# Expert blocks of 96 tokens, with tokens 64 to 95 in four narrow column groups of TensorE

## What the reference computes

```python
logits = (h @ w_router) + b_router
topv, idx = lax.top_k(logits, 4)            # 4 of 32 experts for each of 512 tokens
gates = softmax(topv)
# for each expert e and the tokens x that chose it
gu = x @ w_gate_up[e] + b_gate_up[e]        # 1024 -> 2 x 1024
gate = minimum(gu[:, :1024], 7.0)
up = clip(gu[:, 1024:], -7.0, 7.0)
act = (up + 1.0) * (gate * sigmoid(1.702 * gate))
y = act @ w_down[e] + b_down[e]             # 1024 -> 1024
# out[token] += gate weight * y
```

## Time and profile before

| what | value |
|---|---|
| median of 3 runs | 3157.65 us (3156.02 to 3158.03) |
| profiled execution, from first to last instruction | 3155.9 us |
| median of the runs less that span | 1.75 us |
| TensorE busy in the span | 2956.2 us |
| VectorE, ScalarE, GpSimd busy | 1215.3, 751.5, 116.9 us |
| transfers of expert weights in the span | 384 of 1 MB |

### The profile page before, as it was taken

How to read it: one execution, slowest core, us unless ns; L and a number is a source line. 1 busy time by engine, 2 the same in 40 slices (tenths; PEclk the granted TensorE clock), 3 DMA queues, 4 the chain that set the end, 5 groups by cost and what they waited for, 6 DMA issues and landing times.

```text
span 3155.9 us, 43167 instructions
## 1 busy us (share of the span) xinstructions
PE 2956.2 (94%) x15320; PEld 2056.7 (65%) x15321; DVE 1215.3 (39%) x2572; ACT 751.5 (24%) x1483; POOL 116.9 (4%) x132
## 2 busy tenths in 40 slices
PE   8989899998999999899899879898999999999999
PEld 7874667655585556386357668586776596776774
DVE  6770773242212221211212156535333355444432
ACT  3221751111212121211211023514111225232111
POOL 0000100000000000000000000011000000110000
PEclk9999999988999999999999989899999999999999
DMA  4222012257999999999999452021321220112221
GB/s 171 81 67 79 3 41 80 74 204 298 395 364 365 419 413 390 416 379 382 408 415 391 149 201 95 1 87 49 108 84 54 100 95 27 61 61 87 81 80 67
DMA packets 137804, 577.60 MB, mean 183 GB/s; under 512 B 15981, under 2 KB 21485, under 8 KB 87504
## 3 DMA queue, kind: packets, MB, share of 16 engines
q1 hardware_dynamic: 128176, 558.87, 46.6%
q0 software_dynamic: 9504, 17.07, 1.4%
HBM read 572.47 MB, written 20.97 MB: 188 GB/s over the span
## 4 chain that ended last, share of the span: by engine, by line
PE 85%; DVE 5%; DMA 5%; ACT 2%; issue 2%; DVEq 1%; SPq 0%; POOLq 0%; ACTq 0%
PE banks L395 31%; PE banks L1521 13%; PE banks L1497 9%; PE banks L332 8%; PE banks L1027 7%; PE banks L1471 6%; DMA arena<-in_w_experts 5%; PE banks L800 3%; PE banks L823 2%; PE banks L811 2%; PE banks L271 1%; DVE arena L873 1%; DVE arena L885 1%; PE banks L1451 1%; PE banks L1926 1%
## 5 line engine op out<-in xcount | busy, mean ns | idle before, releaser
L395 PE MATMUL banks<-arena 128*128 128x256 f32 (+2 forms) x4704 | 1015.3, 377 | 21.6 <-ACT arena L432 7.4
L395 PEld LDWEIGHTS banks<-arena 128*128 128x128 f32 x4704 | 883.8, 192 | 142.0 <-issue 21.5
L1521 PEld LDWEIGHTS banks<-arena 128*128 128x128 f32 x3584 | 403.8, 193 | 14.5 <-issue 14.5
L1521 PE MATMUL banks<-arena 128*128 128x128 f32 x3584 | 405.5, 277 | 4.7 <-issue 4.7
L1497 PE MATMUL banks<-arena 128*64 128x512 f32 (+1 forms) x1024 | 322.6, 593 | 0.0
L1471 PE MATMUL banks<-arena 128*64 128x512 f32 x1152 | 268.3, 616 | 24.9 <-DMA arena<-in_w_experts 22.3
L1599 DVE TENSOR_TENSOR arena<-banks,arena 128x512 f32<-128x512 f32 x64 | 44.3, 692 | 614.1 <-PE banks L1521 351.9
L432 ACT ACTIVATE arena<-banks 128x512 f32<-128x512 f32 (+2 forms) x168 | 98.7, 588 | 690.9 <-PE banks L395 690.9
L448 DVE TENSOR_TENSOR arena<-banks,arena 128x512 f32<-128x512 f32 (+2 forms) x126 | 85.7, 680 | 436.2 <-PE banks L395 434.7
L332 PE MATMUL banks<-arena 128*128 128x512 f32 x576 | 250.0, 593 | 0.0
L1497 PEld LDWEIGHTS banks<-arena 128*64 128x64 f32 (+1 forms) x1024 | 123.5, 159 | 176.1 <-issue 176.0
(11 more groups left out here) (210 smaller groups left out, 2041.0 us busy)
## 6 DMA issues: line engine op xcount, KB each, us to landing
arena<-in_w_experts SPq DMA_DIRECT2D x384, 1024.0 KB, 19.3
arena<-in_w_in SPq DMA_DIRECT2D x84, 1024.0 KB, 5.0
arena<-in_w_out SPq DMA_DIRECT2D x12, 1024.0 KB, 5.0
arena<-in_w_branch SPq DMA_DIRECT2D x24, 512.0 KB, 4.7
arena<-expert_rows SPq DMA_DIRECT2D x4, 2048.0 KB, 14.4
arena<-in_w_in SPq DMA_DIRECT2D x4, 832.0 KB, 4.6
arena<-in_gate_b SPq DMA_DIRECT2D x2, 1536.0 KB, 6.5
arena<-in_x SPq DMA_DIRECT2D x4, 512.0 KB, 5.3
```

What stands on the lines that cost most here:

```text
L395: last = PE.matmul(PS[:, bank, t * width:(t + 1) * width], one[:, t * P:(t + 1) * P], other, start=(first and t == 0 and kk == 0), stop=(t ...
L1521: last = PE.matmul(PS[:, q, f * P:(f + 1) * P], gate_up(q, k)[:, f * P:(f + 1) * P], xT[:, k], start=(f == 0 and k == 0), stop=(f == 3 and ...
```

## The change

Blocks hold up to 96 tokens instead of 128, and the table, the places and the lists follow: `LPE` = 6 lists for each expert instead of 4, so `LISTS` is 192, and places are computed with a block size of 96. A block with more than 64 tokens no longer has a path of its own. It takes the path of the short block for its tokens 0 to 63, and beside each of its parts the products of tokens 64 to 95: these 32 tokens are held in four column groups, each 32 wide, and each group is sent other weight columns, 256 at a time. The results lie in four quarters of the partitions of the PSUM banks that are free at that time, and ScalarE copies them out beside the others. The core of the diff:

```diff
-MAXBLK = S * TOPK // P + NE
+BS = 96
+LPE = -(-S // BS)
+WAYS = 1 << 14
+PART = -(-WAYS // BS)
+MAXBLK = S * TOPK // BS + NE
...
-        LISTS = TT * NE
+        LISTS = LPE * NE
...
-                for b in range(TT):
+                for b in range(LPE):
                     V.tensor_tensor(slots[:, :, b], oh, v(R + 1856 + 16 * b, 16).unsqueeze(2).to_broadcast([P, 16, NE]), ALU.mult)
...
-        GU_ = HT + 3072
+        GU_, GV_ = HT + 3072, W + 3072
...
+                    def more_products(h, ks):
+
+                        for k in ks:
+                            for g in range(4):
+                                last = PE.matmul(PS[QB * g:QB * (g + 1), 3 - h, 0:256], xT[:, k, HB:BS],
+                                                 gate_up(2 * h + g // 2, k)[:, 256 * (g % 2):256 * (g % 2) + 256],
+                                                 start=(k == 0), stop=(k == 7), tile_position=(0, QB * g))
+                        return last
+
+                    def turn_products(h, more):
...
+                        if more:
+                            for f in range(2):
+                                for s in range(2):
+                                    half = slice(HB * s, HB * (s + 1))
+                                    to = PS[:, 2 * h + s].rearrange("p (a f t) -> p f a t", a=2, f=2)
+                                    last = PE.transpose(to[:, f, :, HB:BS], v(GV_ + 256 * h + f * P, P, HB, HB * s),
+                                                        ident[half, half])
                         last.then_inc(SEM["gu_rdy"], 1)
...
                             for n in range(2):
-                                to, tokens = place(n)
-                                last = PE.matmul(to, aT[:, f, 0:tokens], down_rows(f)[:, n * 512:(n + 1) * 512],
-                                                 start=(f == 0), stop=(f == 7))
+                                last = PE.matmul(PS[HB * n:HB * (n + 1), 6 + n], aT[:, f, 0:HB],
+                                                 down_rows(f)[:, n * 512:(n + 1) * 512], start=(f == 0), stop=(f == 7))
                             if f % 2 == 1:
+                                if more:
+                                    for ff in (f - 1, f):
+                                        for g in range(4):
+                                            last = PE.matmul(PS[QB * g:QB * (g + 1), 7 - g // 2, 0:256], aT[:, ff, HB:BS],
+                                                             down_rows(ff)[:, 256 * g:256 * g + 256],
+                                                             start=(ff == 0), stop=(ff == 7), tile_position=(0, QB * g))
                                 last.then_inc(SEM["ch_free"], 1)
...
+                    def rows_of_block(more):
                         for h in range(2):
                             for kh in range(2):
+                                ks = range(4 * kh, 4 * kh + 4)
                                 arrived(part(2 * h, 4 * kh))
                                 arrived(part(2 * h + 1, 4 * kh))
                                 if h and kh:
-                                    turn_products(0)
-                                products(h, range(4 * kh, 4 * kh + 4)).then_inc(SEM["ch_free"], 2)
-                        turn_products(1)
+                                    turn_products(0, more)
+                                last = products(h, ks)
+                                if more:
+                                    last = more_products(h, ks)
+                                last.then_inc(SEM["ch_free"], 2)
+                        turn_products(1, more)
                         gather_T(j + 2)
-                        down(lambda n: (PS[HB * n:HB * (n + 1), 6 + n], HB))
+                        down(more)
+
+                    with pe.If(few > 0):
+                        rows_of_block(False)
                     with pe.Else():
-                        held = 0
...
+                        rows_of_block(True)
...
-                            AC.activation(v(GU_ + 512 * h, 512), PS[:, 4 + h], ACT.Copy).then_inc(SEM["gu_out"], 1)
+                            last = AC.activation(v(GU_ + 512 * h, 512), PS[:, 4 + h], ACT.Copy)
+                            if more:
+                                last = AC.activation(v(GV_ + 256 * h, 256), PS[:, 3 - h, 0:256], ACT.Copy)
+                            last.then_inc(SEM["gu_out"], 1)
                             gate(h)
                         copy_T(j + 2)
                         rows_ready()
                         AC.activation(v(Y_, 512, HB), PS[0:HB, 6], ACT.Copy)
-                        AC.activation(v(Y_ + 512, 512, HB), PS[HB:P, 7], ACT.Copy).then_inc(SEM["y_rdy"], 1)
+                        last = AC.activation(v(Y_ + 512, 512, HB), PS[HB:P, 7], ACT.Copy)
+                        if more:
+                            for g in range(4):
+                                last = AC.activation(v(Y_ + 256 * g, 256, QB, HB), PS[QB * g:QB * (g + 1), 7 - g // 2, 0:256], ACT.Copy)
+                        last.then_inc(SEM["y_rdy"], 1)
```

More of the change, by code:

```diff
@@ L1222, in router_stage @@
             addr = v(R + 1696, 16).bitcast(I32)
-            at_p, at_b = v(R + 1760, 16).bitcast(I32), v(R + 1776, 16).bitcast(I32)
+            at_b = v(R + 1776, 16).bitcast(I32)
             row_f, blk_f = v(R + 1808, 16), v(R + 1824, 16)
             rows_at = v2(W, 16, P)
-            slots = v3(HT + 1024, 16, TT, NE)
+            slots = v3(HT + 1024, 16, LPE, NE)
             brow = v(R + 1728, NE)
@@ L1258, in pe_ @@
                 pe.wait_ge(SEM["column_rdy"], up(1))
-                for q, col in enumerate((TAB + 352, TAB + 356, TAB + 357)):
+                for q, col in enumerate((FOUND, FOUND + 4, FOUND + 5)):
                     last = PE.matmul(PS[0:1, 1, 64 * q:64 * q + 64], v(col, 1), ident[:, 0:64], start=True, stop=True)
@@ L1332, in dve_ @@
                 cnt, nb, cum = v(TAB, NE), v(TAB + 32, NE), v(TAB + 64, NE)
[L1333 to L1338, removed]
+                t1 = v2(TAB + 96, NE, LPE)
+                step = v(TAB + 96 + NE * LPE, NE)
+                past = v2(TAB + 128 + NE * LPE, 3, NE)
+                found = v(FOUND, 3)
+                bef, stf, left = (v(FOUND + q, 1) for q in range(3))
+                of, few, row = v(FOUND + 4, 1), v(FOUND + 5, 1), v(FOUND + 6, 1)
                 V.tensor_copy(cnt, PS[:, 1, 128:160])
@@ L1420, in expert_stage @@
             J = MAXBLK + 2
-            HB = P // 2
+            HB, QB = P // 2, P // 4
             def nblocks(eng):
@@ L1482, in turn_products, with down @@
                                                     v(GU_ + 512 * h + f * P, P, HB, HB * s), ident[half, half])
+                        if more:
[5 more added lines that the diff above has]
+                                                        ident[half, half])
                         last.then_inc(SEM["gu_rdy"], 1)
-                    def down(place):
+                    def down(more):
                         pe.wait_ge(SEM["y_rdy"], up(j))
@@ L1507, in pe_ @@
                                 if h and kh:
-                                    turn_products(0)
-                                products(h, range(4 * kh, 4 * kh + 4)).then_inc(SEM["ch_free"], 2)
-                        turn_products(1)
+                                    turn_products(0, more)
[4 more added lines that the diff above has]
+                        turn_products(1, more)
                         gather_T(j + 2)
-                        down(lambda n: (PS[HB * n:HB * (n + 1), 6 + n], HB))
+                        down(more)
+                    with pe.If(few > 0):
+                        rows_of_block(False)
                     with pe.Else():
-                        held = 0
[L1515 to L1521, removed]
-                                                             xT[:, k], start=(f == 0 and k == 0), stop=(f == 3 and k == 7))
-                                            if held:
-                                                last.then_inc(SEM["ch_free"], 1)
-                                                held = 0
-                                    if kh and q % 2:
-                                        last.then_inc(SEM["gu_rdy"], 1)
-                                        held = 1
-                                    else:
-                                        last.then_inc(SEM["ch_free"], 1)
-                        gather_T(j + 2, free=1)
-                        down(lambda n: (PS[:, 6 + n], P))
+                        rows_of_block(True)
             def act_(act, c):
@@ L1555, in rows_ready, with rows_of_block @@
                         apart(act, j)
-                    with act.If(few > 0):
+                    def rows_of_block(more):
                         for h in range(2):
@@ L1565, in act_ @@
                         AC.activation(v(Y_, 512, HB), PS[0:HB, 6], ACT.Copy)
```

(14 more changed lines are left out.)

30 lines of the change are left out of this document (13 added, 17 removed).

## The result

The changed kernel took 3114.69 us, median of 4 runs (3111.05 to 3118.27), the kernel before 3156.84 (3153.43 to 3158.03) on the same chip: a ratio of 0.9869, 95% interval 0.9857 to 0.9881, or 42 us less. Forecast were 47 less. The profiled executions are the slowest of either kernel (3158.03 before; 3118.27 after, span 3116.4), and the two traces differ by 39.5 us only.

What follows compares the result with a forecast made beforehand. TensorE was taken as busy 94%, with expert weights' pace as the floor close below. Block 29 at 1645.9 plus three 36.8 us blocks ends at 1756.3 against 1804.9; with +1.7 tail, -47: 3111 us, range 3100 to 3150.

Steps and rivals of the forecast that it cites:

- Four groups at once: Long block's narrow products: four column groups run concurrently, 6.9 us gate and up, 3.5 down; 0.61 with weights as floor.
- two show no loss at all: Argument for four groups: 32 records of 64-wide products take 7.02 us, where 32 of full width take 13.78.
- two at a time: Rival: narrow products run only in pairs, a long block takes 47.2 us, about 3200 us in all; chance 0.15.
- Exposed loads: Rival: narrow weight loads do not overlap matmuls, 6.7 us more a long block, about 3160 us; chance 0.04.
- Changes of width: Long block on TensorE: 14 added changes of column-group width at 0.13 us each, 1.8 us in all.
- The long block: Expert block of more than 64 tokens on TensorE: 36.8 us after the change, against 43.2 before.
- The weights as floor: Expert loop: weight chunks land no faster than one per 2.707 us, 32.5 us a block, at 418 GB/s.
- TensorE alone: Rival: TensorE alone sets the time, weights could come faster: -85 us, 3073 us in all; chance 0.02.
- The router: Before the expert loop: larger lists add 2.7 us to list products; first gather and everything after start 3.0 us later.
- The tail: After the last expert block: ScalarE's additional copies out of PSUM add 1.7 us before the last scatter.
- start of block 29: First of the last three long blocks starts at 1645.9 us, when its second weight chunk, number 337, is there.
- blocks 29 to 31: Last three expert blocks, all long: 3 x 36.8 us, ending at 1756.3 us, where it was 1804.9 before.

Runs made afterwards that it cites:

- run 4: Changed kernel with narrow products reordered by pairs of column groups (0 and 1 for all k, then 2 and 3): 3146.09 us.
- run 5: Also one_by_one: changed kernel with narrow products reordered, all k of one column group, then the next group: 3222.14 us.
- Run 7: Changed kernel with narrow products put before wide ones in each part of a long block's down products: 3113.83 us, ratio 0.9861 to the kernel before.
- run 1: Changed kernel with products, transposes and copies for tokens 64 to 95 left out of long blocks: 3091.63 us, against 3153.60 for the kernel before.
- run 2: Changed kernel with each weight transfer in the expert loop bringing only the first half of its chunk: 3037.89 us.
- run 3: Kernel before the change with each weight transfer in the expert loop bringing only the first half of its chunk: 3115.80 us.
- run 6: Changed kernel with narrow products reordered so each column group gets two k, four records, in a row: 3115.93 us.
- run 10: Changed kernel with 2 router lists for each expert instead of 6: 3111.83 us, ratio 0.9856 to the kernel before.
- run 12: Changed kernel with narrow down products first and four gathered-row transposes moved ahead of the second turn: 3108.31 us, ratio 0.9837 to the kernel before.
- again: Changed kernel measured once more, unchanged: 3110.81 us, ratio 0.9851 to the kernel before.

## Why the prediction was right, point by point

- **Four groups at once.** Right: 32 records take 8 x 0.216 us. It rested on "two show no loss at all", and what carries it was not in that argument: the order in which the kernel sends the records, two records for each group in turn, so that no group is full while another is idle. That the kernel had such an order was luck. In another order the same products cost 3.5 or 10.5 us a block more (runs 4 and 5). The rival "two at a time" was wrong: even the order in pairs takes 41.2 us a block, not 47.2. The 0.057 us that a transpose takes was no measure of how closely records can start: the four groups start 0.007 us apart.
- **Exposed loads.** Wrong, as forecast. The 32-wide loads of L1481 take 109 ns each and come in eight sets of four. If nothing ran beside them they would add 8 x 0.109 = 0.87 us to the 8 x 0.216 = 1.73 of a step's records; the step takes 1.87. The Trainium skill ("TensorE: Matmul & The Clock Gate", Part 3), by which loads overlap only across row groups, is not what this trace shows: these share all rows and overlap.
- **Changes of width.** Forecast 0.13 each; measured 3.59 - 16 x 0.2155 = 0.14 for the wide step, 1.87 - 8 x 0.216 = 0.14 for the narrow one.
- **The long block.** Forecast 36.8, measured 37.7. The missing 0.9 is the [0.94 <-issue] ahead of the next block, a term that the sum lacks: behind 593 ns records no gap shows, behind 16 short ones it does. Run 7 takes it away with one change of order. The wait for ScalarE grew by 0.29, from 0.88 to 1.17, forecast 0.4.
- **The weights as floor.** Right (runs 1 to 3; the last chunk but one lands at 1738.0, where the last was forecast, and 404 GB/s move for the 418 forecast), and the step on which the forecast stands: without it the gain would have been near 78 us, as the rival "TensorE alone" (85) had it.
- **The router.** Between the two profiles the list products grew from 5.28 to 8.19 us: forecast +2.7, measured +2.9. The gather starts 5.6 us later, forecast 3.0; the other 2.5 lie ahead of the list products, which start at 703.10 for 700.64. That is not the change: the kernel before in run 3, whose router is untouched, starts them at 703.35 too, and takes 6.54 us for them, at a granted clock of 0.56 where the profile of before has 0.70. So this part varies by 1 to 3 us from one execution to the next, and the share of the lists in it is 1.7 to 2.9. A gather 1.9 shorter takes part of it back, and block 0 starts 3.7 us later.
- **The tail.** Last product's end to last scatter 4.0 us for 2.25, +1.8; forecast +1.7. After (timeline, ScalarE's three steps and then the scatter on GpSimd):

```profile
1761.14 1.07 PE L1520 MATMUL banks<-arena 128*32 128x256 f32 x16
1762.52 0.59 ACT L1580 ACTIVATE arena<-banks 64x512 f32<-64x512 f32 x1 [9.79 <-PE banks L1520]
1763.12 0.59 ACT L1581 ACTIVATE arena<-banks 64x512 f32<-64x512 f32 x1
1763.73 1.53 ACT L1584 ACTIVATE arena<-banks 32x256 f32<-32x256 f32 x4
1766.23 1.01 POOL L1649 DMA_INDIRECT expert_rows<-arena  x1 [13.47 <-ACT arena L1584]
```

The sum, by its steps:

| step | forecast | profile | difference |
|---|---|---|---|
| start of block 29 | 1645.9 | 1649.7 | +3.8 |
| blocks 29 to 31 | 110.4 | 112.5 | +2.1 |
| tail | +1.7 | +1.8 | +0.1 |
| what follows the experts | 0 | +1.5 | +1.5 |
| whole | -47 | -39.5 | +7.5 |

The first line is a landing 1.1 later at the loop's fourth chunk (742.8 for 733.6 + 3 x 2.707 = 741.7), 334 chunks at 2.712 for 2.707 us (+1.7) and 1 us of waits; the second is mostly the gap between blocks, which comes twice here (1.00 and 0.95). The fourth is seen in the chain of waits, where the way from the first projection records behind the experts to the long run of them (1803.96 to 1813.16) is 9.2 us long. Before it was 7.5:

```profile
1844.76 2.00 PE banks L395 x8
...
1852.28 65.85 PE banks L395 x304
```

The eight records took 3.39 us at a granted clock of 0.56, and 2.00 at 1.00 before. In runs 6, 7, 10 and 12 the changed kernel's variants take 1.99 for them and in again it is 3.55, so this part comes with the execution and not with the change. The median of the runs is 3.6 us better than that profile, and before it is 1.2 better, so 42 of 47 us came. No step failed; the one that was mis-sized by a mechanism is the long block, by 0.9. One slip is in the range: at about 3160 the exposed loads lie outside it too, so it leaves out 0.24 and not 0.20.

## What to carry to other kernels

A record with 128 held float32 columns took 0.112 us with 128 sent past it and with 96. So a few tokens more were cheap only as the held side, in as many column groups as fit, and with at most four records of a group in a row. Before an engine's work is cut, ask what comes next: here nearly half of 78 us went to the transfer of weights, and further cuts of TensorE's time (runs 7, 12) could count in the last three blocks alone and gave nothing clear of the noise. End a loop's body with its longest instructions: with short ones there 0.94 us between blocks stayed open (run 7).

## What the runs showed of the hardware that was not expected

- **Four records a group.** A column group takes four matmul records, one running and three waiting; a fifth blocks those behind it for other groups too (0.89 us each time in runs 4 and 5, nothing with four in run 6 and in the down part). That a fifth is what blocks is worked out from the starts; the costs of the other orders follow from it. Starts are not in the program's order: in one_by_one the second group's first record starts at 0.894 us, the first group's sixth to eighth, sent ahead of it, later. The Trainium skill ("TensorE: Matmul & The Clock Gate", Part 3) has matmuls start and end strictly in order; across column groups this trace does not agree.
- **The first pass through a code path.** The first long block waits 7.00 us for "issue" at 750.06 after, 4.7 before, 5.0 in again, 3.3 with half of the weights' traffic and 1.6 where the long path is short. It was longer with full traffic and with a long path, but it also differs by 2 us between two executions of the changed kernel. In 748 to 757 us the profile's DMA queue of kind "instruction" moves 0.03 MB in two packets after and 0.02 in one with the short path; that their arrival is what TensorE waits for was not tested, and the cause stays open.
- **A cheaper step that is hardly faster.** In run 10 a third of the columns saved 1.2 us of 8.25, at a granted clock of 0.50 for 0.63 in the stretch around it.
